# Differential attention: unscaled first map, one maximum for both maps, four probability buffers

## The reference

```
def attend(qb, keys, vals):
    s = jnp.einsum('bhmtd,bhmsd->bhmts', pair(qb), keys).astype(f32) * DIFF_DH ** -0.5
    p = jax.nn.softmax(s, axis=-1)
    a = (p[:, :, 0] - lam * p[:, :, 1]).astype(vals.dtype)
    return jnp.einsum('bhts,bhse->bhte', a, vals)

def finish(o):
    Bt, _, Lt, _ = o.shape
    o = rmsnorm(o, subln) * (1.0 - lambda_init)
    return o.transpose(0, 2, 1, 3).reshape(Bt, Lt, DIFF_HEADS * 2 * DIFF_DH) @ w_out

keys = pair(jnp.concatenate([kc, k], axis=2))
vals = jnp.concatenate([vc, v], axis=2)
y = finish(sweep_query_blocks(lambda qb: attend(qb, keys, vals), q))
yc = finish(attend(qc, pair(kc), vc)) if ctx_out else None
```

## Time and profile before

| | us |
|---|---|
| median of 3 executions | 2293.82 |
| lowest, highest | 2290.10, 2298.74 |
| the profiled execution | 2299.57 |
| its span in the trace | 2297.5 |
| mean granted clock in it | 0.955 |
| busy in the span: PE, DVE, ACT, POOL | 2147.2, 1325.3, 931.1, 103.9 |

### The profile page before, as it was taken

How to read it: one execution, slowest core, us unless ns; L and a number is a source line. 1 busy time by engine, 2 the same in 40 slices (tenths; PEclk the granted TensorE clock), 3 DMA queues, 4 the chain that set the end, 5 groups by cost and what they waited for, 6 DMA issues and landing times.

```text
span 2297.5 us, 34461 instructions
## 1 busy us (share of the span) xinstructions
PE 2147.2 (93%) x13918; PEld 1886.5 (82%) x13918; DVE 1325.3 (58%) x2081; ACT 931.1 (41%) x1376; POOL 103.9 (5%) x156
## 2 busy tenths in 40 slices
PE   3999998999899998988999999798999999898999
PEld 1998797998899987668997997476878788777997
DVE  2677767677736775537665754864222333855444
ACT  2434435344523445435345544653222232554343
POOL 1000000000100001100001000002000000200000
PEclk7999999999879998989999999998999999999999
DMA  8697765987368775645864221023433223305553
GB/s 290 229 318 259 267 239 186 306 285 254 122 216 297 276 255 175 243 173 189 271 218 155 93 92 56 1 92 100 157 127 129 92 92 101 101 29 202 183 174 119
DMA packets 246603, 411.40 MB, mean 179 GB/s; under 512 B 10221, under 2 KB 191942, under 8 KB 246470
## 3 DMA queue, kind: packets, MB, share of 16 engines
q1 hardware_dynamic: 246470, 409.54, 52.0%
HBM read 408.47 MB, written 1.05 MB: 178 GB/s over the span
## 4 chain that ended last, share of the span: by engine, by line
PE 82%; DVE 8%; DMA 3%; ACT 3%; POOL 2%; issue 2%; SPq 0%; DVEq 0%; ACTq 0%; POOLq 0%
PE bank L1796 19%; PE bank L1745 15%; PE bank L1746 14%; PE bank L1747 14%; PE bank L1852 3%; PE bank L1853 3%; PE bank L1854 3%; DMA ada<-in_ada_w 3%; PE bank L1712 2%; PE bank L1888 1%; PE bank L1731 1%; DVE astat L1507 1%; DVE w_lo L1107 1%; PE bank L1975 1%; POOL h_lo L674 1%
## 5 line engine op out<-in xcount | busy, mean ns | idle before, releaser
L1107 DVE TENSOR_TENSOR w_lo<-stage,w_hi 128x2048 fp32r<-128x2048 f32 x255 | 585.5, 2297 | 553.8 <-ACT w_hi L722 553.2
L1745 PE MATMUL bank<-h_hi,w_hi 128*128 128x256 f32 (+1 forms) x2432 | 741.6, 305 | 25.1 <-POOL h_lo L674 18.6
L722 ACT CAST w_hi<-stage 128x2048 fp32r<-128x2048 f32 x255 | 485.2, 1904 | 634.0 <-PE bank L1747 249.1
L1746 PE MATMUL bank<-h_lo,w_hi 128*128 128x256 f32 (+1 forms) x2432 | 734.3, 302 | 0.0
L1747 PE MATMUL bank<-h_hi,w_lo 128*128 128x256 f32 (+1 forms) x2432 | 733.9, 302 | 0.0
L1745 PEld LDWEIGHTS bank<-h_hi,w_hi 128*128 128x128 f32 x2432 | 474.3, 195 | 53.4 <-issue 35.6
L1746 PEld LDWEIGHTS bank<-h_lo,w_hi 128*128 128x128 f32 x2432 | 474.4, 195 | 15.3 <-issue 1.9
L1747 PEld LDWEIGHTS bank<-h_hi,w_lo 128*128 128x128 f32 x2432 | 473.9, 195 | 14.1
L1796 PE MATMUL bank<-w_hi,h_hi 128*128 128x512 f32 x776 | 245.6, 394 | 9.3 <-DVE h_lo L1116 8.8
L1796 PE MATMUL bank<-w_lo,h_hi 128*128 128x512 f32 x776 | 244.0, 391 | 0.0
L1796 PE MATMUL bank<-w_hi,h_lo 128*128 128x512 f32 x776 | 243.7, 391 | 0.0
(11 more groups left out here) (210 smaller groups left out, 1949.6 us busy)
## 6 DMA issues: line engine op xcount, KB each, us to landing
ada<-in_ada_w SPq DMA_DIRECT2D x120, 1024.0 KB, 5.6
stage<-in_ffn_w_in SPq DMA_DIRECT2D x88, 1024.0 KB, 8.6
stage<-in_ffn_w_out SPq DMA_DIRECT2D x44, 1024.0 KB, 5.1
stage<-in_ffn_w_gu SPq DMA_DIRECT2D x44, 1024.0 KB, 5.1
stage<-in_ffn_w_down SPq DMA_DIRECT2D x22, 1024.0 KB, 4.9
stage<-in_a_w_in SPq DMA_DIRECT2D x12, 1024.0 KB, 8.6
stage<-in_diff_w_in SPq DMA_DIRECT2D x12, 1024.0 KB, 5.1
ada<-in_kv_ada_w SPq DMA_DIRECT2D x8, 1024.0 KB, 5.9
```

Source lines behind the costliest of these rows:

```text
L722: a.copy(w_hi[:, s, :], stage[:, s, :]).then_inc(hi_done, 1)
L1107: v.tensor_tensor(w_lo[:, s, :], stage[:, s, :], w_hi[:, s, :].bitcast(F32), ALU.subtract).then_inc(lo_done, 1)
L1745: m.matmul(dst[:, 0:T], wh, h_hi[:, h0:h0 + T], start=(k == ks[0]), stop=False)
L1746: m.matmul(dst[:, 0:T], wh, h_lo[:, h0:h0 + T], start=False, stop=False)
```

## The change

In the loop:

- `probs_d` gets two more pairs of buffers, in `gate_b`. Job J uses pair J % 4, and its exponentials wait for the transposes of J - 4.
- The maxima of both maps are one instruction over the two banks, which gives them negated. The instruction that negated them is gone. It waits for the combination of J - 4 too, since the place of its result comes round every four jobs.
- The first map isn't scaled any more. With d0 and d1 the sums of the two maps, the combination is e0 - lambda * (d0 / d1) * e1, that is, d0 times what it was. The reciprocal is of d1 alone, and the coefficient is a two-input instruction with d0.
- The sums go to a place of their own in `ada_row`, two for each of the 32 jobs, since d0 is needed at the end.

At the end, the norm makes good for the factor: with o' = d0 * o, the result is o' / sqrt(mean(o'^2) + 1e-6 * d0^2). VectorE squares the 32 values of d0 (one more instruction), and the mean becomes sum + 128e-6 * d0^2, with the 1/128 in the scale of ScalarE's root.

```diff
--- before.py
+++ after.py
@@ -359,6 +359,19 @@
         diff_jobs = [(h, tt, 0 if tt < 2 else 2) for h in range(8) for tt in range(4)]
         gqa_jobs = [(h, tt, 0) for h in range(8) for tt in range(2)]
         probs_d = [[mid[:, 8192 + b * D + m_ * 512:8192 + b * D + (m_ + 1) * 512] for m_ in range(2)] for b in range(2)]
+        probs_d += [[gate_b[:, b, m_ * 512:(m_ + 1) * 512] for m_ in range(2)] for b in range(2)]
+
+        def d_max(J, m_=slice(0, 2)):
+            return flat_astat[:, J % 4 * 8:J % 4 * 8 + 2][:, m_]
+
+        def d_coef(J):
+            return flat_astat[:, J % 4 * 8 + 2:J % 4 * 8 + 3]
+
+        def d_inv(J):
+            return flat_astat[:, J % 4 * 8 + 3:J % 4 * 8 + 4]
+
+        def d_den(J, m_):
+            return ada_row[:, 128 + 2 * J + m_:129 + 2 * J + m_]
         aT_d = [mid[:, 10240 + b * 512:10240 + (b + 1) * 512] for b in range(2)]
         probs_g = [mid[:, 6144 + b * 512:6144 + (b + 1) * 512] for b in range(2)]
         pT_g = [mid[:, 7168 + b * 512:7168 + (b + 1) * 512] for b in range(2)]
@@ -973,11 +986,11 @@
                         h, tt, k0 = jobs[J]
                         b, nk = J % 2, (4 - k0) * P
                         act.wait_ge(dve_s, t.at((tag, "neg", J)))
-                        if J >= 2:
-                            act.wait_ge(pe_s, t.at((tag, "jt", J - 2)))
+                        if J >= 4:
+                            act.wait_ge(pe_s, t.at((tag, "jt", J - 4)))
                         for m_ in range(2):
-                            ins = a.activation(probs_d[b][m_][:, 0:nk], bank[2 * b + m_][:, 0:nk], ACT.Exp,
-                                               bias=astat[:, b, 1, m_:m_ + 1], accum_out=astat[:, b, 2, m_:m_ + 1])
+                            ins = a.activation(probs_d[J % 4][m_][:, 0:nk], bank[2 * b + m_][:, 0:nk], ACT.Exp,
+                                               bias=d_max(J, slice(m_, m_ + 1)), accum_out=d_den(J, m_))
                         t.done(ins, act_s, (tag, "exp", J))
                     if 0 <= J - 2 < len(jobs):
                         i = J - 2
@@ -994,7 +1007,7 @@
                             act.wait_ge(dve_s, t.at((tag, "osum", h - 2)))
                         t.done(a.activation(silu_t[:, h % 2, :], w.qT[:, h, :], ACT.Square), act_s, (tag, "osq", h))
                 act.wait_ge(dve_s, t.at((tag, "omean")))
-                t.done(a.activation(ada_row[:, 64:96], ada_row[:, 32:64], ACT.Sqrt), act_s, (tag, "oroot"))
+                t.done(a.activation(ada_row[:, 64:96], ada_row[:, 32:64], ACT.Sqrt, scale=1.0 / P), act_s, (tag, "oroot"))
                 gate(s, tag, 0)
                 for h in range(8):
                     act.wait_ge(pe_s, t.at((tag, "ot", h)))
@@ -1503,28 +1516,28 @@
                         h, tt, k0 = jobs[J]
                         b, nk = J % 2, (4 - k0) * P
                         dve.wait_ge(pe_s, t.at((tag, "s", J)))
-                        for m_ in range(2):
-                            ins = v.reduce_max(astat[:, b, 0, m_:m_ + 1], bank[2 * b + m_][:, 0:nk], AX_X)
-                        t.done(ins, dve_s, (tag, "max", J))
-                        dve.wait_ge(dve_s, t.at((tag, "max", J)))
-                        t.done(v.tensor_scalar(astat[:, b, 1, 0:2], astat[:, b, 0, 0:2], -1.0, None, ALU.mult), dve_s, (tag, "neg", J))
+                        if J >= 4:
+                            dve.wait_ge(dve_s, t.at((tag, "p", J - 4)))
+                        t.done(v.reduce_max(d_max(J), bank_all[:, 2 * b:2 * b + 2, 0:nk], AX_X, negate=True), dve_s, (tag, "neg", J))
                     if 0 <= J - 1:
                         i = J - 1
-                        b, nk = i % 2, (4 - jobs[i][2]) * P
-                        p0, p1 = probs_d[b][0][:, 0:nk], probs_d[b][1][:, 0:nk]
+                        nk = (4 - jobs[i][2]) * P
+                        p0, p1 = probs_d[i % 4][0][:, 0:nk], probs_d[i % 4][1][:, 0:nk]
                         dve.wait_ge(act_s, t.at((tag, "exp", i)))
-                        t.done(v.reciprocal(astat[:, b, 3, 0:2], astat[:, b, 2, 0:2]), dve_s, (tag, "inv", i))
+                        t.done(v.reciprocal(d_inv(i), d_den(i, 1)), dve_s, (tag, "inv", i))
                         dve.wait_ge(dve_s, t.at((tag, "inv", i)))
-                        t.done(v.tensor_scalar(astat[:, b, 4, 0:1], astat[:, b, 3, 1:2], NEG_LAM, None, ALU.mult), dve_s, (tag, "coef", i))
-                        t.done(v.tensor_scalar(p0, p0, astat[:, b, 3, 0:1], None, ALU.mult), dve_s, (tag, "p0", i))
-                        dve.wait_ge(dve_s, t.at((tag, "p0", i)))
-                        t.done(v.scalar_tensor_tensor(out=p0, in0=p1, scalar=astat[:, b, 4, 0:1], in1=p0, op0=ALU.mult, op1=ALU.add), dve_s, (tag, "p", i))
+                        t.done(v.scalar_tensor_tensor(out=d_coef(i), in0=d_inv(i), scalar=NEG_LAM, in1=d_den(i, 0), op0=ALU.mult, op1=ALU.mult), dve_s, (tag, "coef", i))
+                        dve.wait_ge(dve_s, t.at((tag, "coef", i)))
+                        t.done(v.scalar_tensor_tensor(out=p0, in0=p1, scalar=d_coef(i), in1=p0, op0=ALU.mult, op1=ALU.add), dve_s, (tag, "p", i))
                     if J >= 8 and J % 4 == 0:
                         osum((J - 8) // 4)
                 gate(s, tag, 0)
+                d0 = ada_row[:, 128:192].rearrange("p (j m) -> p j m", m=2)[:, :, 0]
+                t.done(v.tensor_tensor(ada_row[:, 32:64], d0, d0, ALU.mult), dve_s, (tag, "d2"))
                 osum(7)
                 dve.wait_ge(dve_s, t.at((tag, "osum", 7)))
-                t.done(v.tensor_scalar(ada_row[:, 32:64], ada_row[:, 0:32], 1.0 / P, EPS, ALU.mult, ALU.add), dve_s, (tag, "omean"))
+                dve.wait_ge(dve_s, t.at((tag, "d2")))
+                t.done(v.scalar_tensor_tensor(out=ada_row[:, 32:64], in0=ada_row[:, 32:64], scalar=EPS * P, in1=ada_row[:, 0:32], op0=ALU.mult, op1=ALU.add), dve_s, (tag, "omean"))
                 dve.wait_ge(act_s, t.at((tag, "oroot")))
                 t.done(v.reciprocal(ada_row[:, 96:128], ada_row[:, 64:96]), dve_s, (tag, "oinv"))
                 dve.wait_ge(dve_s, t.at((tag, "oinv")))
@@ -2038,7 +2051,7 @@
                     if 0 <= J - 2 < len(jobs):
                         i = J - 2
                         h, tt, k0 = jobs[i]
-                        src, dst = (probs_d[i % 2][0], bank[4 + i % 2]) if w.diff else (probs_g[i % 2], bank[2 + i % 2])
+                        src, dst = (probs_d[i % 4][0], bank[4 + i % 2]) if w.diff else (probs_g[i % 2], bank[2 + i % 2])
                         pe.wait_ge(dve_s, t.at((tag, "p", i)))
                         if i >= 2:
                             pe.wait_ge(act_s, t.at((tag, "evT", i - 2)))
```

## The result

| | before | changed |
|---|---|---|
| median of 10 executions | 2296.76 | 2286.34 |
| lowest, highest | 2290.10, 2305.39 | 2279.83, 2296.48 |
| ratio to before, 95% interval | | 0.9948 [0.9930, 0.9965] |
| predicted ratio | | 0.9945 |
| the loop, first maximum to last product | 93.35 | 79.65 |

By the ratio the gain is 11.9 us (8.0 to 16.1) of 2296.76, and the interval reaches over the 0.5% line on both sides. Timed once more with the last experiments, the changed kernel came to 0.9931 [0.9910, 0.9952], 2282.61 against 2297.35. The two intervals overlap. The loop's own 13.7 us would be a ratio of 0.994, which lies in both.

A forecast was written before the change was run, and what follows sets the result against it. VectorE's chain was taken to bound the differential loop, then the ScalarE path at 9.55 us a head. Heads summed to 12.6 us saved, profiled 2299.57 to 2287.0, ratio 0.9945, median 2293.82 to 2281.2; range 2274 to 2290.

The forecast's parts named there:

- What bounds the loop: In the differential loop (93.35 us), VectorE's closed chain bounds a head at 11.15 us; a shorter loop ends the kernel earlier.
- One maximum, negated: One reduction over both maps: 1.216 us for 1024 elements, 0.68 for 512; negation priced at zero; 0.26 saved a job.
- The unscaled map: Combination 0.25 us behind the coefficient; dropping the scaling saves 0.26 for 256-key jobs, 0.39 for 512-key jobs.
- What is late next: After the cut, the path through ScalarE bounds a full-clock head at 9.55 us, so it falls 1.60, not 2.4.
- the way over ScalarE: Head's path through second job's exponentials, then last job's copy, product and scores on TensorE: 9.55 us, before 10.34.
- the predicted way over VectorE: Closed loop of VectorE's first three steps, then TensorE's transposes, product and next scores: 9.33 us a head.
- Four buffers at zero: Exponentials waiting four jobs back, not two: counted zero, covered by the maximum; without cover 0.1 a head, 0.8 in all.
- Sum over the heads: Savings over the loop's eight heads: 11.5 us with every low-clock stretch, 14.0 with none; 12.6 taken.
- rival 2: TensorE's low clock goes: all 14 us and some more, 2278 to 2280; chance 0.16, the semaphore rule's 0.03 included.
- Rivals 1, 3 and 4: More handoff waits (0.25); clock stays 1.2 GHz, 2296 to 2311 (0.04); no effect or hidden later, 2290 to 2294 (0.05).
- clock in the loop below 0.9: A granted clock below 0.9 in the differential loop would make the prediction wrong on the slow side.
- rival 1: More waits between engines in the loop: heads of 10.2 us and more, gain 6 to 10, 2284 to 2288; chance 0.25.

## Why the prediction was right, point by point

- **What bounds the loop:** right. The loop lost 13.7 us and the kernel 11.9 (8.0 to 16.1); the work behind it didn't take it back. It took 793.36 before, 795.64 and 794.28 in two executions of the changed kernel, and between 791 and 795 in the others.
- **One maximum, negated:** 1.220 and 0.687 us for 1024 and 512 elements, the means over the loop, 1.216 and 0.68 predicted; two results and the negation cost nothing that shows. The reciprocal stands 1.14 behind its start, as worked out.
- **The unscaled map:** 0.26 from coefficient to combination, 0.25 predicted. Here the rule of the Trainium skill (VectorE: DVE Perf Modes, "The DRAIN you can't avoid") that a semaphore costs nothing extra would have given 0.13. The trace goes with the row and against the rule: on VectorE an instruction that waits for its forerunner starts 0.03 to 0.04 behind its end, one that doesn't 0.08 ahead of it.
- **What is late next:** right in place and size for the way over ScalarE (9.53 for 9.55), and shown by taking the exponentials out of it. What that freed was half of what was expected, because the predicted way over VectorE came to 9.43 and not 9.33, with A's product at 1.06 for 0.98. A third way, over A's transposes, was missed; it lies close to these two and changed nothing in the forecast.
- **Four buffers at zero:** 0.06 to 0.07 a head by undoing them, 0.46 in the last head and 1.0 in all, for "0.1 a head, 0.8 in all" without cover. The step that failed a little is the claim that the maximum covers the transposes fully: with two buffers C's exponentials start 0.16 later, and the way on, over A's copy to A's product, was not looked at.
- **Sum over the heads:** head 0 gave 0.4 (0.7 predicted, and 0.23 in the second execution), head 1 2.15 (1.5, or 2.3 with the clock), heads 2, 3, 5 and 6 1.61 to 1.63 each (1.6), head 4 2.43 (1.6 or 2.4), head 7 2.22 (1.3 or 2.2; 12.18 for 12.2). That is 13.7, close to the upper end, 14.0, since all low stretches behind head 0 went. The middle, 12.6, was too careful. This part of rival 2 came true. That the low stretches were absent in both executions of the changed kernel and in every kernel with heads up to 10.31, and came back with the padding, speaks for TensorE's waits as the cause, and against mere luck. The sum itself left this open between 11.5 and 14.0.
- **Rivals 1, 3 and 4:** no handoff was more than 0.02 off; the clock rose (0.96 for 0.91 over the loop) instead of falling; nothing behind the loop is seen to absorb the gain. The sign "clock in the loop below 0.9" did not appear.
- **The number:** 0.9945 predicted, 0.9948 and 0.9931 measured. With intervals of about 0.002 to either side, an agreement to 0.0003 is luck; what was right is the size of the loop's gain and what bounds it. In microseconds the median, 2286.34, lies among those of rival 1 (2283 to 2289), but the kernel before measured 2296.76 beside it and not 2293.82, and by the ratio the forecast's 2281.2 became 2281.9. Whether the gain lies beyond the 0.5% line stays open. The first profile alone, 3.1 us shorter than before, would have spoken for "hidden"; the loop's own time didn't.

## What to carry to other kernels

Where three engines pass small pieces round, write down every closed way from one step to the same step a period later, with the start-to-start times of the trace, and take the longest; cutting work on the busiest engine pays only down to the second longest, here 1.62 of 2.34 us. Then look whether the ways can be cut by more lag instead: with the buffers there, a job more between combination and transposes, and copies ahead of exponentials, gave another 1.18 a head for no work removed. And compare the stretch that was changed, not the spans of two executions, when an untouched stage scatters by as much as the effect.

## What the runs showed of the hardware that I had not expected

- With TensorE's own work unchanged, more waiting brought the low clock (1.2 GHz) into most heads of a loop: two extra VectorE instructions a job took the loop's granted clock from 0.96 to 0.77, and the step in which it is low from 2.54 to 5.02 us. Padding that lengthened three steps of a head by 1.67 us in all cost the head 4.15 (13.68 to 9.53).
- The same code in the sparse attention ran at granted clocks of 0.84 to 0.94 from execution to execution, worth 14 us between the extremes (97.3 and 111.5 us from its first product to its last, loop starts at 1405.02 and 1419.11).
- One VectorE reduction over two PSUM banks costs just the fixed part and 1.04 ns an element, as if it were one (1.220 us for 1024, where the rows of 512 and 256 give 1.216), with no price for crossing the bank.
